# Between three scans of a token mixer: order of the last units, key lengths by block products, closing norms placed in the next scan

## The reference, cut to what matters

```python
y = unboth(_ssd_chunked(...)) + ssd_d[:, None] * xs
y_ssd = _rmsnorm_groups(y * silu(z), ssd_norm_w, 256)
kk = k * rwkv_kk
kk = kk / maximum(sqrt(sum(kk * kk, -1)), 1e-12)          # per head of 64
a_f = sigmoid(a0[0] + ad_f @ a2[0])                        # a_b likewise
w_f = exp(-exp(-softplus(-(w0[0] + tanh(wd_f) @ w2[0])) - 0.5))
k_f = k * (1.0 + (a_f - 1.0) * ka)
y = unboth(_rwkv7_scan(r, w, k, v, kk, a))                 # delta rule
y_gla = _rmsnorm_groups(o, gla_norm_w, 64) * silu(og)      # o from _gla_chunked
return concatenate([y_ssd, y_rwkv, y_gla], -1) @ w_out
```

## Time and profile before

| what | value |
|---|---|
| median of 3 runs | 2976.57 us (2973.63 to 2979.05) |
| the profiled execution | 2973.56 us, span 2971.8 us |
| busy: PE, PEld, DVE, ACT, POOL | 94%, 72%, 59%, 38%, 7% of the span |
| mean granted TensorE clock | 0.963 |

### The profile page before, as it was taken

How to read it: one execution, slowest core, us unless ns; L and a number is a source line. 1 busy time by engine, 2 the same in 40 slices (tenths; PEclk the granted TensorE clock), 3 DMA queues, 4 the chain that set the end, 5 groups by cost and what they waited for, 6 DMA issues and landing times.

```text
span 2971.8 us, 41823 instructions
## 1 busy us (share of the span) xinstructions
PE 2778.9 (94%) x16898; PEld 2130.0 (72%) x16898; DVE 1741.3 (59%) x3174; ACT 1130.0 (38%) x2004; POOL 207.7 (7%) x211
## 2 busy tenths in 40 slices
PE   7998887878999999999988998999999997999998
PEld 4887765776566776666655775888888775788887
DVE  4257866665677778776646687433333688433333
ACT  3322233223145556555532327432222326432222
POOL 0000000000012222222210030000000030000000
PEclk9999887889999999999999999999999999999999
DMA  6210001322449889999977240222323250222412
GB/s 228 85 57 22 1 1 45 108 72 88 166 171 351 345 341 361 350 358 343 346 283 296 94 111 12 85 93 92 115 66 117 93 131 19 85 72 78 142 54 74
DMA packets 186542, 442.38 MB, mean 149 GB/s; under 512 B 21283, under 2 KB 110694, under 8 KB 167014
## 3 DMA queue, kind: packets, MB, share of 16 engines
q1 hardware_dynamic: 161862, 396.59, 37.1%
q0 software_dynamic: 24480, 43.04, 4.9%
HBM read 426.43 MB, written 38.29 MB: 156 GB/s over the span
## 4 chain that ended last, share of the span: by engine, by line
PE 67%; DVE 8%; DMA 5%; ACT 3%; issue 2%; POOL 0%; SPq 0%; POOLq 0%; ACTq 0%; DVEq 0%
PE ps L296 15%; PE ps L298 15%; PE ps L297 15%; PE ps L2496 6%; DMA ring<-in_ew 3%; PE ps L2012 2%; PE ps L1504 2%; PE ps L2522 1%; DMA hg<-h_rows,idx 1%; PE ps L2735 1%; DVE Pb L3482 1%; PE ps L2216 1%; PE ps L3387 1%; DMA yr<-y_rows 1%; PE ps L1561 1%
## 5 line engine op out<-in xcount | busy, mean ns | idle before, releaser
L2947 DVE TENSOR_TENSOR wf<-ring,wf 128x1024 fp32r<-128x1024 f32 (+1 forms) x152 | 181.7, 1196 | 310.5 <-ACT wf L2943 310.2
L2943 ACT ACTIVATE wf<-ring 128x1024 fp32r<-128x1024 f32 (+1 forms) x152 | 156.8, 1033 | 343.3 <-PE ps L298 343.3
L296 PE MATMUL ps<-hxh,wf 128*128 128x512 f32 (+1 forms) x736 | 280.7, 381 | 2.3 <-DVE hxl L3110 2.3
L297 PE MATMUL ps<-hxl,wf 128*128 128x512 f32 (+1 forms) x736 | 280.2, 381 | 0.0
L298 PE MATMUL ps<-hxh,wf 128*128 128x512 f32 (+1 forms) x736 | 280.2, 381 | 0.0
L2434 DVE TENSOR_TENSOR spA<-ring,spA 128x1024 fp32r<-128x1024 f32 x156 | 184.4, 1221 | 106.7 <-ACT spA L2429 106.6
L2496 PE MATMUL ps<-ring,hdT 128*128 128x512 f32 x520 | 234.8, 594 | 0.8 <-issue 0.8
L2429 ACT ACTIVATE spA<-ring 128x1024 fp32r<-128x1024 f32 x156 | 157.6, 1053 | 60.0 <-DMA ring<-in_ew 54.2
L2496 PEld LDWEIGHTS ps<-ring,hdT 128*128 128x128 f32 x520 | 93.8, 190 | 94.3 <-issue 90.7
L2434 DVE TENSOR_TENSOR spB<-ring,spB 128x1024 fp32r<-128x1024 f32 x104 | 124.0, 1221 | 62.6 <-ACT spB L2429 62.3
L296 PEld LDWEIGHTS ps<-hxh,wf 128*128 128x128 f32 x736 | 139.2, 189 | 28.8 <-DVE hxl L3110 2.8
(11 more groups left out here) (618 smaller groups left out, 6184.7 us busy)
## 6 DMA issues: line engine op xcount, KB each, us to landing
ring<-in_ew SPq DMA_DIRECT2D x65, 2048.0 KB, 12.4
ring<-in_ew SPq DMA_DIRECT2D x65, 1024.0 KB, 6.7
ring<-in_w_in SPq DMA_DIRECT2D x17, 2048.0 KB, 7.9
ring<-in_w_gate SPq DMA_DIRECT2D x20, 1024.0 KB, 5.4
ring<-in_w_up SPq DMA_DIRECT2D x20, 1024.0 KB, 7.9
ring<-in_w_down SPq DMA_DIRECT2D x16, 1024.0 KB, 5.0
adaw<-in_ada_w SPq DMA_DIRECT2D x24, 512.0 KB, 6.5
ring<-in_w_out SPq DMA_DIRECT2D x6, 2048.0 KB, 9.6
```

Source lines behind the costliest of these rows:

```text
L296: pe.matmul(o, lhs[0], rhs[0], start=start, stop=False)
L297: pe.matmul(o, lhs[0], rhs[1], start=False, stop=False)
L2943: act.activation(item_part(n)[0], item_raw(n), ACT.Copy).then_inc(*w_hi.inc(n))
L2947: v.tensor_tensor(item_part(n)[1], item_raw(n), f(item_part(n)[0]), ALU.subtract).then_inc(*w_lo.inc(n))
```

## The change

- The weave becomes four strands: forward SSD and behind it `rwset`, forward GLA, backward SSD, backward GLA; so GLA's last units stand behind one short step of `rwset` per round. In `gla_dve` the last unit yields once more after its clamp.
- Key lengths: squares come straight from the keys (`rwm`), are summed over a head and spread by one product with a block matrix of ones (`h64`), then `Ln` and `Exp(-0.5 x)` give the reciprocal root, and one VectorE instruction takes the minimum with 1e12 and the product. The tanh of the decay input goes to the end of the projection. `kd_` is half done on ScalarE (`Identity` with scale and bias).
- `glan` keeps one Square and one gate product. The rest of both norms is a new strand `mixn` of the second weave, with `Ln` and `Exp` for roots, all its transposes in PSUM bank 6 that the modulation steps use.
- Two of the four SSD gate products move into `ssd_dve`.
- `ADAT` loses 13 and gains 54. A few buffers move.

The norm functions that it removes (`ssdn_*`, the old `glan_*`) stand in full above and are left out below.

```diff
+                if n == 16:
+                    act.activation(rwm[:, 6, :], rwm[:, 6, :], ACT.Tanh).then_inc(*b_evA.inc(("tanh", 0)))
...
+                if i == 4:
+                    v.wait_ge(*PV.val((u, "yd")))
+                    v.tensor_tensor(ydst, ydst, zx[:, b6 - 2, :], ALU.mult).then_inc(*V.inc())
...
                 v.tensor_scalar(cq, ga[:, 0:128], 640.0, -640.0, ALU.min, ALU.max).then_inc(*Gd.inc((u, "cq")))
+                if i == 5:
+                    yield
...
     def glan_act(act):
-        act.wait_ge(*g_dve[0].val(((5, 0), "o")))
-        act.wait_ge(*g_dve[1].val(((5, 1), "o")))
+        act.wait_ge(*s_dve[0].val(((5, 0), "yd")))
+        for d in range(2):
+            act.wait_ge(*g_dve[d].val(((5, d), "o")))
+        act.activation(gsq, og2f, ACT.Square).then_inc(*z_act.inc("gsq"))
+        yield
...
+    def glan_dve(v):
+        for d in range(2):
+            v.wait_ge(*g_dve[d].val(((5, d), "o")))
+        v.tensor_tensor(gat, og2f, ogt[:, :, :].rearrange("p i n -> p (i n)"), ALU.mult).then_inc(*z_dve.inc("gate"))
+        yield
...
+    def mixn_pe(pe):
+        yield from rest(6)
+        for n in range(6):
+            if n:
+                pe.wait_ge(*z_dve.val(("ymg", n - 1) if n < 3 else ("ym", n - 3)))
+            pe.wait_ge(*z_dve.val("gn" if n < 2 else ("yn", n - 2)))
+            for k in range(4):
+                src = gat[:, 256 * (2 * n + k % 2) + 128 * (k // 2):256 * (2 * n + k % 2) + 128 * (k // 2) + 128] if n < 2 else \
+                    yn[n % 2][:, k * 128:(k + 1) * 128]
+                m = pe.transpose(ps[6][:, k * 128:(k + 1) * 128], src, ident)
+            m.then_inc(*z_pe.inc(n))
+            yield
+            yield
...
+    def mixn_act(act):
+        act.wait_ge(*x_dve.val(("zx", 3)))
         for i in range(4):
-            act.activation(gsq[i], og2[:, i, :], ACT.Square).then_inc(*n_act.inc(("sq", i)))
+            for g in range(2):
+                at = 1024 + 512 * i + 256 * g
+                act.activation(uf[:, at:at + 256], ysd[:, i, g * 256:(g + 1) * 256], ACT.Square,
+                               accum_out=mvS[:, i, g:g + 1]).then_inc(*(z_act.inc(("sq", i)) if g else S.inc()))
...
+        act.wait_ge(*z_dve.val("gsum"))
+        act.activation(mvG[:, 1, :], mvG[:, 0, :], ACT.Ln, bias=EPS5, scale=1.0 / 64).then_inc(*S.inc())
+        act.wait_ge(*S.val())
+        act.activation(mvG[:, 1, :], mvG[:, 1, :], ACT.Exp, scale=-0.5).then_inc(*z_act.inc("grs"))
         yield
-        for i in range(4):
-            act.wait_ge(*n_dve.val(("sum", i)))
-            act.activation(mvG[:, i, 4:8], mvG[:, i, 0:4], ACT.Sqrt, bias=EPS5, scale=1.0 / 64).then_inc(*n_act.inc(("sd", i)))
+        act.wait_ge(*z_act.val(("sq", 3)))
+        act.activation(mvS[:, :, 2:4], mvS[:, :, 0:2], ACT.Ln, bias=EPS5, scale=1.0 / 256).then_inc(*S.inc())
+        act.wait_ge(*S.val())
+        act.activation(mvS[:, :, 4:6], mvS[:, :, 2:4], ACT.Exp, scale=-0.5).then_inc(*z_act.inc("srs"))
...
+        v.wait_ge(*z_act.val("gsq"))
+        v.tensor_reduce(mvG[:, 0, :], gsq.rearrange("p (h v) -> p h v", v=64), AX.X, ALU.add).then_inc(*z_dve.inc("gsum"))
+        yield from rest(4)
+        v.wait_ge(*z_act.val("grs"))
+        v.wait_ge(*z_dve.val("gate"))
+        v.tensor_tensor(gat.rearrange("p (h v) -> p h v", v=64), gat.rearrange("p (h v) -> p h v", v=64), bc(mvG[:, 1, :], 64),
+                        ALU.mult).then_inc(*z_dve.inc("gn"))
+        yield
+        yn_(0)
+        yield
+        ymg(0)
...
+        def lora(n):
+            _, q, h = AH8[n]
+            lo, w = HALVES[h]
+            if n:
+                pe.wait_ge(*x_act.val(AH8[n - 4] if n >= 4 else "ln"))
+            pe.matmul(ps[abank[n]][:, 0:w], a2x[:, q * 128:(q + 1) * 128], rwm[:, 7, lo:lo + w]).then_inc(*x_pe.inc(AH8[n]))
...
+        for d in range(2):
+            pe.wait_ge(*s_dve[d].val(((5, d), "ys")))
+        pe.wait_ge(*d_rw.val("in"))
+        lora(0)
+        yield
+        yield
+        for p in (1, 0):
+            pe.wait_ge(*x_act.val(("sq", p)))
+            pe.matmul(ps[p][:, :], C("h64"), sqk[:, p, 0:512])
+            m = pe.matmul(ps[2][:, 256 * p:256 * p + 256], C("h64"), sqk[:, p, 512:768])
         m.then_inc(*x_pe.inc("kk"))
         yield
...
+        for n in range(1, 4):
+            lora(n)
         yield
-
-        pe.wait_ge(*x_act.val("tanh"))
+        for n in (4, 6):
+            lora(n)
+            lora(n + 1)
+            yield
+
+        pe.wait_ge(*b_evA.val(("tanh", 0)))
         for b6 in range(6):
...
     def rwset_act(act):
-        for p in range(2):
-            act.wait_ge(*x_dve.val(("kk", p)))
-            act.activation(sqk[p], kkT[:, p, :], ACT.Square).then_inc(*x_act.inc(("sq", p)))
+        for d in range(2):
+            act.wait_ge(*s_pe[d].val(((5, d), "o")))
+        for p in (1, 0):
+            act.activation(sqk[:, p, :], rwm[:, 2 + p, :], ACT.Square, scale=cc("kk", p)).then_inc(*x_act.inc(("sq", p)))
+        yield
+        act.wait_ge(*x_dve.val(("zx", 0)))
+        for p in (1, 0):
+            act.activation(kkT[:, p, :], rwm[:, 2 + p, :], ACT.Copy, scale=cc("kk", p)).then_inc(*x_act.inc(("kk", p)))
         yield
         act.wait_ge(*x_pe.val("kk"))
-        act.activation(rns, ps[2][:, 0:24], ACT.Sqrt).then_inc(*x_act.inc("sd"))
+        act.activation(sqk[:, :, 0:512], psa[:, 0:2, :], ACT.Ln, bias=TINY).then_inc(*S.inc())
+        act.activation(sqk[:, :, 512:768], ps[2].rearrange("p (q t) -> p q t", q=2), ACT.Ln, bias=TINY).then_inc(*x_act.inc("ln"))
+        act.wait_ge(*S.val())
+        act.wait_ge(*x_act.val("ln"))
+        act.activation(xpad[:, 0:1536], xpad[:, 0:1536], ACT.Exp, scale=-0.5).then_inc(*x_act.inc("rn"))
+        yield
         for d in range(2):
-            act.wait_ge(*s_pe[d].val(((5, d), "o")))
             act.wait_ge(*s_dve[d].val(((5, d), "yd")))
-        for q in range(4):
-            for h, (lo, n) in enumerate(HALVES):
-                act.wait_ge(*x_pe.val(("a", q, h)))
-                act.activation(aT[:, q, lo:lo + n], ps[3 - h][:, 0:n], ACT.Sigmoid, bias=cc("a0", q)).then_inc(*x_act.inc(("a", q, h)))
-            yield
-        act.activation(th, rwm[:, 6, :], ACT.Tanh).then_inc(*x_act.inc("tanh"))
-        yield
+        for n, k in enumerate(AH8):
+            _, q, h = k
+            lo, w = HALVES[h]
+            act.wait_ge(*x_pe.val(k))
+            act.activation(aT[:, q, lo:lo + w], ps[abank[n]][:, 0:w], ACT.Sigmoid, bias=cc("a0", q)).then_inc(*x_act.inc(k))
+            if h:
+                yield
         for b6 in range(6):
             act.wait_ge(*x_pe.val(("lw", b6)))
             at = 2 * (b6 % 2)
             act.activation(lw[:, b6, :].rearrange("p (d n) -> p d n", d=2), psa[:, at:at + 2, 0:256],
                            ACT.Sigmoid).then_inc(*x_act.inc(("lw", b6)))
+            if b6 < 4:
+                act.wait_ge(*x_act.val(("a", b6, 1)))
+                if b6 == 3:
+                    for d in range(2):
+                        act.wait_ge(*g_pe[d].val(((5, d), "cum")))
+                act.activation(kd_[:, b6, :], aT[:, b6, :], ACT.Identity, bias=omka[:, b6 % 2:b6 % 2 + 1],
+                               scale=cc("ka", b6 % 2)).then_inc(*x_act.inc(("kd", b6)))
...
     def rwset_dve(v):
-        v.wait_ge(*s_dve[1].val(("zx", 3)))
-        for p in range(2):
-            v.tensor_scalar(kkT[:, p, :], rwm[:, 2 + p, :], cc("kk", p), None, ALU.mult).then_inc(*x_dve.inc(("kk", p)))
+        for d in range(2):
+            v.wait_ge(*s_dve[d].val(((5, d), "yd")))
+        for i in (0, 3):
+            v.tensor_tensor(ysd[:, i, :], ysd[:, i, :], zx[:, i, :], ALU.mult).then_inc(*x_dve.inc(("zx", i)))
+        yield
+        v.wait_ge(*x_dve.val(("zx", 3)))
         v.memset(Hr[:, :, :, :], 0.0).then_inc(*V.inc())
-        yield
-        v.wait_ge(*x_act.val("sd"))
-        v.tensor_scalar(rns, rns, 1e-12, None, ALU.max).then_inc(*V.inc())
-        v.wait_ge(*V.val())
-        v.reciprocal(rns, rns).then_inc(*x_dve.inc("rn"))
-        yield
-        v.wait_ge(*s_act[1].val(("sq", 3)))
-        for q in range(4):
-            p = q % 2
-            v.wait_ge(*x_act.val(("a", q, 1)))
-            if q == 3:
-                for d in range(2):
-                    v.wait_ge(*g_pe[d].val(((5, d), "cum")))
-            v.tensor_scalar(kd_[:, q, :], aT[:, q, :], -1.0, cc("ka", p), ALU.add, ALU.mult).then_inc(*V.inc())
-            v.wait_ge(*V.val())
-            v.scalar_tensor_tensor(out=kd_[:, q, :], in0=kd_[:, q, :], scalar=1.0, in1=rwm[:, 2 + p, :], op0=ALU.add,
-                                   op1=ALU.mult).then_inc(*V.inc())
+        yield from rest(3)
+        v.wait_ge(*x_act.val(("kk", 0)))
+        v.wait_ge(*x_act.val("rn"))
+        kf = kkT[:, :, :].rearrange("p q t -> p (q t)")
+        v.scalar_tensor_tensor(out=kf, in0=xpad[:, 0:1536], scalar=1e12, in1=kf, op0=ALU.min, op1=ALU.mult).then_inc(*x_dve.inc("rn"))
+        yield from rest(3)
```

(72 more changed lines are left out.)

189 lines of the change are left out of this document (39 added, 150 removed).

## The result

| | before | changed |
|---|---|---|
| median beside each other | 2977.81 us (4 runs, 2973.63 to 2986.85) | 2950.82 us (4 runs, 2947.86 to 2956.71) |
| ratio | | 0.9905, 95% interval 0.9886 to 0.9925 |
| timed again, on the chip of the last experiments | 2977.89 us (7 runs) | 2952.55 us (4 runs) |
| ratio there | | 0.9912, interval 0.9895 to 0.9928 |
| profiled execution, span | 2973.56, 2971.8 | 2956.71, 2954.9 |

Faster by some 0.9%: the medians differ by 27 us, where the prediction said 2945 and 31 us less. The ratios are the measurement's own estimates; the quotients of the medians are 0.9909 and 0.9915.

A forecast was written before the change was run, and what follows sets the result against it. Between the scans nothing is full and a chain bounds the kernel. Part 1, -42, and Part 2, +11, sum to -31: profiled 2973.56 becomes 2942.6, median named 2945, own range 2935 to 2955, wider 2930 to 2962.

The forecast's parts named there:

- The forecast case: Whole kernel: time between the scans saved, part of the norms paid in the delta-rule scan, 2945 us; chance 0.62.
- the tail of part 1: End of the set-up: six decay groups paced by ScalarE, 6.8 us to 446.9, then VectorE's products until 449.9.
- Part 1: Between the SSD and GLA scans and the delta-rule scan: work removed and reordered, -42 us, bounds -27 and -46.
- The term for the two moved products: Two gate products moved into the SSD scan, 0.7 us each on VectorE; 1.0 us added.
- The 2 us that the prediction gave back for half clock: Between the scans: 2 us given back for stretches at half clock; longest TensorE idle time some 3 us, under the Ln.
- Part 2: Norms inside the delta-rule scan's first unit, rounds 1 to 18: +11 us, bounds +4 and +24.
- The sum by that rule, -36: Ln and Exp pairs need one load each: Part 2 some 4 us less, Part 1 one less, sum -36.
- Norms hidden: Delta-rule scan: the norms cost only +2 to +4 us, giving 2937; chance 0.15.
- Half clock between the scans: TensorE's wait for the Ln keeps the clock at 1.2 GHz, -27 + 11, giving 2960; chance 0.09.
- Norms in full: Delta-rule scan: in-order waits pass on all 24 us of the norms, giving 2958; chance 0.07.
- Units not first: Between the scans: a key set-up wait still precedes GLA's last unit, half the 42 lost, 2966; chance 0.04.
- Slower: Delta-rule scan: ScalarE's first-unit stall drops the clock and it stays down, 90 us more, 3035; chance 0.03.

The follow-up runs named there:

- f4: Changed kernel with the decay products on all 128 rows instead of 64; 2955.67 us, one execution, 35.1 us between the scans against 37.6.
- e4: Changed kernel with all four SSD gate products behind the scan, none in it; 2943.24 us, one execution, 137.8 us up to SSD end against 140.0.
- e1: Changed kernel with both Ln of the closing norms in one step, then both Exp, two table loads instead of four; 2942.70 us, first unit 36.8 against 40.3.
- e2: Changed kernel with Square in place of the closing norms' Ln and Exp, so no table loads there; first unit 36.6 us against 40.3, total 3036.20 with other routing.
- e3: Changed kernel with the closing norms run by themselves ahead of the delta-rule scan; 2951.63 us, one execution, 56.6 us between the scans, scan 226.8.
- f2: Kernel before with seven unread 512-column matmuls filling TensorE's idle time after the last SSD add; 74.4 us between the scans against 78.5, scan 227.6.
- f1: Changed kernel with GLA's last unit held back six rounds on all three engines; 2963.63 us, one execution, 50.8 us between the scans against 37.6.

## Why the prediction was right, and where it was off

The forecast case came in: faster by 0.95% by the ratio, the median 2950.8 inside 2930 to 2962 and inside the forecast's own 2935 to 2955. By the sums from the set-up's load to the output weights, before 447.7 and 447.0, changed 416.5 and 416.4, the change is worth 30.9 us, where the prediction had 31. That it comes so near is luck: two misses of almost 3 us cancel. The mechanism was right in the main, but for the tail of part 1. Point by point:

- **Part 1, -42.** Measured up to the scan's first copy: 216.3 and 217.1 before, 177.5 and 177.5 changed, so -39.2. Three terms were off. The term for the two moved products was 1.0 and is 2.0 ("up to SSD end" is 140.1 on average with them and 138.1 without, seven profiles and six, f4's left out, whose 143.4 would make it 2.4; 2.2 in e4), with the clock behind the wait in it. From 493.28 to 450.9 are 42.4 us; the prediction made 44 of them "with the second strand's", but the first copies of the two strands are 2.2 us apart in both kernels, so this 1.6 was nothing. The third, and the step that failed, is the tail: "six decay groups, 1.27 on TensorE and 0.6 on ScalarE each ... ScalarE sets the pace", then "VectorE's tail is late next". The last three of the six groups ran at half clock for 2.3 us each, TensorE set their pace (ScalarE's last sigmoid waited 1.71 us), and VectorE then idled for 3.36 us until the decays' exponential. f4 puts 2.4 us on it. The 2 us that the prediction gave back for half clock covered most of this by luck, with another place in mind, under the Ln. That wait didn't come (0.19 us). 1.6, 1.0 and 2.4 less those 2 make 3.0, close to the 2.8 missed.
- **Part 2, +11.** The scan took 231.4 and 229.9 us before, 239.0 and 238.9 changed: +8.3. The loads cost what was forecast, 3.7 (3.8 of ScalarE's time; 3.5 of the unit with e1, 3.7 with e2). The rest was priced at 6.9 and shows as 4.5 or 8.4, depending on the scan without norms that one takes: the kernels before, or e3, whose scan has 226.8. f2 too has 227.6 with nothing changed but matmuls ahead of it, so the same scan's length varies by some 4 us; what from isn't shown, and which of the two is its own time stays open. The first unit alone, 40.3 against 33.3, is +7.0; the forecast had 8 to 11. The other five, forecast as long as before, took 198.7 and 198.6 against 198.1 and 196.7.
- The two misses, 2.8 less gained and 2.7 less paid, cancel. The range took in the bounds of each part only with the other part at its forecast: -27 and +24 together would have been 2974.
- **Loads and the rule.** An Exp to Ln step costs a load and the step back another, everywhere in the changed kernel: the trace's reading stood. The Trainium skill, "ScalarE: Activation LUTs", section "Table sets: the hidden batching unit", has both functions in one set; here no pair went with one load, and the measurement decides. The sum by that rule, -36, would have missed by 5.
- **Median.** Of the 30.9 us, 27.0 and 25.3 show in the two pairs of medians. The code from the expert stage on is the same, and took 2134.9 and 2135.0 us in e3 and e4, 2133.9 in the first profile of before, but 2143.1 in the second; the changed kernel took 2146.4 twice, and f4 the same. So it is not slowed by the change as such (e3 and e4 each keep all of it but one part), and it varies by 17 us over these profiles. Whether the changed kernel as it stands falls on its long side more often is not settled by so few.
- **The rivals.** Norms hidden (2937): no, 8.3 us show. Half clock between the scans (2960): the clock did fall to 0.50, which the prediction had named as a sign of being wrong, but at 446 us, for the last quarter, and not for its reason, TensorE's wait for the Ln. Norms in full (+24): no, in series they cost 19.0 and in the scan 8.3 to 12.2. Units not first: no, "cum" came at once; f1 shows what another order would have cost, 13.2 us. Slower: the first unit's mean clock was 0.75 against 0.78, the second's 0.91 against 0.94. Behind the wait under the loads the clock was at 0.67 for 5 us (480 to 485) and then back at 1.00.
